# Keys and values of the latent attention by three passes over high and low halves, and two search rounds moved

## The reference, cut to what matters

```python
q, c, qi, ki, wi = jnp.split(h @ w_in, ATT_IN_SPLITS, axis=-1)   # c: 512 x 128, the latent
c = rms_norm(c, kv_norm_g)
score = einsum('bqh,bqhs->bqs', wi, relu(einsum('bqhd,bsd->bqhs', qi, ki)))  # causal
_, idx = lax.top_k(score, 128)                 # 128 keys for every query
logits = (q @ w_uk) @ c[idx] * 64**-0.5 + bias  # 16 heads, softmax over the chosen keys
o = (softmax(logits) @ c[idx]) @ w_uv ; out = o @ w_o
```

## Time and profile before

| | |
|---|---|
| median of three runs | 1879.57 us (1879.13 to 1879.93) |
| the profiled execution, its own time | 1879.85 us |
| its span, first to last instruction | 1878.6 us |
| mean granted TensorE clock | 0.999 |
| TensorE busy | 1859.6 us (99%) |
| VectorE busy | 977.0 us (52%) |
| ScalarE busy | 674.3 us (36%) |
| GpSimd busy | 379.9 us (20%) |

### The profile page before, as it was taken

How to read it: one execution, slowest core, us unless ns; L and a number is a source line. 1 busy time by engine, 2 the same in 40 slices (tenths; PEclk the granted TensorE clock), 3 DMA queues, 4 the chain that set the end, 5 groups by cost and what they waited for, 6 DMA issues and landing times.

```text
span 1878.6 us, 21854 instructions
## 1 busy us (share of the span) xinstructions
PE 1859.6 (99%) x8896; PEld 1505.6 (80%) x8900; DVE 977.0 (52%) x1318; ACT 674.3 (36%) x912; POOL 379.9 (20%) x339
## 2 busy tenths in 40 slices
PE   9999999999999999999999999999999999999998
PEld 8888888888877568888888878788787888888887
DVE  7885533334458864543434347666446454443432
ACT  6753322222234772321212334555323332222213
POOL 2004210010336793210101131111001311110103
PEclk9999999999999999999999999999999999999999
DMA  4323322322322103223223222222232322233221
GB/s 159 113 90 90 112 90 93 109 90 91 107 96 93 66 1 112 90 90 112 90 91 111 76 91 90 68 68 68 84 117 79 112 88 93 90 101 101 90 95 62
DMA packets 167171, 172.36 MB, mean 92 GB/s; under 512 B 7480, under 2 KB 164288, under 8 KB 167072
## 3 DMA queue, kind: packets, MB, share of 16 engines
q1 hardware_dynamic: 164576, 163.76, 26.9%
q0 software_dynamic: 2496, 7.21, 1.2%
HBM read 168.69 MB, written 2.14 MB: 91 GB/s over the span
## 4 chain that ended last, share of the span: by engine, by line
PE 86%; DVE 6%; ACT 4%; issue 2%; DMA 0%; POOL 0%; SPq 0%; DVEq 0%; ACTq 0%
PE bank L775 27%; PE bank L777 27%; PE bank L776 27%; DVE wlo L1700 1%; DVE XC L1802 1%; PE bank L800 1%; ACT whi L1218 1%; PE bank L994 1%; PE bank L1096 1%; PE bank L973 1%; ACT pt L1438 0%; PE bank L922 0%; DVE qe L2106 0%; DMA xtok<-in_x 0%; PE bank L1163 0%
## 5 line engine op out<-in xcount | busy, mean ns | idle before, releaser
L775 PE MATMUL bank<-Ahi,whi 128*128 128x512 f32 (+2 forms) x1416 | 552.8, 390 | 2.5 <-DVE wlo L1700 0.8
L776 PE MATMUL bank<-Alo,whi 128*128 128x512 f32 (+2 forms) x1416 | 547.8, 387 | 0.0
L777 PE MATMUL bank<-Ahi,wlo 128*128 128x512 f32 (+2 forms) x1416 | 547.8, 387 | 0.0
L1700 DVE TENSOR_TENSOR wlo<-stage,whi 128x2048 fp32r<-128x2048 f32 (+2 forms) x146 | 333.1, 2281 | 380.3 <-ACT whi L1218 380.3
L1218 ACT ACTIVATE whi<-stage 128x2048 fp32r<-128x2048 f32 (+2 forms) x152 | 287.1, 1889 | 443.3 <-PE bank L777 443.3
L775 PEld LDWEIGHTS bank<-Ahi,whi 128*128 128x128 f32 (+1 forms) x1416 | 265.3, 187 | 65.6 <-issue 8.2
L776 PEld LDWEIGHTS bank<-Alo,whi 128*128 128x128 f32 (+1 forms) x1416 | 265.4, 187 | 54.9 <-issue 1.2
L777 PEld LDWEIGHTS bank<-Ahi,wlo 128*128 128x128 f32 (+1 forms) x1416 | 265.3, 187 | 55.0
L775 PE MATMUL bank<-Hhi,whi 128*128 128x512 f32 x688 | 267.7, 389 | 0.0
L777 PE MATMUL bank<-Hhi,wlo 128*128 128x512 f32 x688 | 267.6, 389 | 0.0
L776 PE MATMUL bank<-Hlo,whi 128*128 128x512 f32 x688 | 267.6, 389 | 0.0
(11 more groups left out here) (349 smaller groups left out, 2145.4 us busy)
## 6 DMA issues: line engine op xcount, KB each, us to landing
stage<-in_mlp_w_up SPq DMA_DIRECT2D x32, 1024.0 KB, 5.3
stage<-in_mlp_w_down SPq DMA_DIRECT2D x32, 1024.0 KB, 4.9
stage<-in_w_in SPq DMA_DIRECT2D x22, 1024.0 KB, 4.9
stage<-in_w_ffn_in SPq DMA_DIRECT2D x22, 1024.0 KB, 4.9
stage<-in_w_ffn_out SPq DMA_DIRECT2D x8, 1024.0 KB, 5.0
stage<-in_rec_w_in SPq DMA_DIRECT2D x7, 1024.0 KB, 5.1
stage<-in_att_w_in SPq DMA_DIRECT2D x6, 1024.0 KB, 5.3
stage<-in_rec_w_out SPq DMA_DIRECT2D x4, 1024.0 KB, 4.6
```

The lines of the kernel that those rows point to most:

```text
L775: e.matmul(ps, hi, rh, start=first, stop=False)
L776: e.matmul(ps, hi, rl, start=False, stop=False)
L777: return e.matmul(ps, lo, rh, start=False, stop=last)
L1700: e.tensor_tensor(lo_of(u)[:, 0:nk, 0:n], stage[s][:, 0:nk, 0:n], f32(hi_of(u)[:, 0:nk, 0:n]), ALU.subtract).then_inc(s_lo[s], 1)
```

## The change

The latent `cT`, the transposed `w_uk` and the weights `w_uv` get high and low halves, and the 8 key products and the 8 value products go by `three` in place of one 32-bit matmul each. ScalarE makes the high halves: `uvh` (128 x 1024) ahead of the copies of `gv`, `chi` (128 x 512) in step m = 1, and `ukh` (2 x 128 x 512) where it made `ukT`. GpSimd makes `uvl` behind unit 50's low half. VectorE makes `clo` at m = 2 and the two `ukl` at m = 3, after two search rounds; the banks of `uk` are now freed by these two instructions. In the loop over m the rounds are 36 in place of 38, and the two left over go to steps 20 and 21 of the attention, the mask from step 20 to step 22.

```diff
@@ buffers
-    ukT = pool("ukT", 102, [128, 8, 128])
+    chi, clo = pool("chi", 82, [128, S], R), pool("clo", 80, [128, S], R)
+    ukh, ukl = pool("ukh", 102, [128, 8, 128], R), [pool("ukl", kb, [128, 4, 128], R) for kb in (98, 30)]
+    uvh, uvl = pool("uvh", 26, [128, 16, 64], R), pool("uvl", 94, [128, 16, 64], R)
@@ GpSimd, behind lo(50)
+        e.wait_ge(s_uvh, 1)
+        e.tensor_tensor(uvl[:, :, :], w_uv[:, :, :], f32(uvh[:, :, :]), ALU.subtract).then_inc(s_uvl, 1)
@@ TensorE
-        e.wait_ge(s_c, 1)
+        e.wait_ge(s_cl, 1)
         e.wait_ge(*ring.free(("uk", 0)))
         e.wait_ge(*ring.free(("uk", 1)))
         for c in range(8):
             ps = begin(("K", c))
-            e.matmul(ps[:, :], ukT[:, c, :], cT[:, :], start=True, stop=True).then_inc(*ring.put(("K", c)))
+            three(ps[:, :], ukh[:, c, :], ukl[c // 4][:, c % 4, :], chi[:, :], clo[:, :], True, True).then_inc(*ring.put(("K", c)))
...
-                e.wait_ge(s_uv, 16)
-            e.matmul(ps[:, :], cT[:, j * 128:(j + 1) * 128], w_uv[:, 8 * i:8 * i + 8, :].rearrange("p h v -> p (h v)"),
-                     start=True, stop=True).then_inc(*ring.put(("val", j, i)))
+                e.wait_ge(s_uvl, 1)
+            three(ps[:, :], chi[:, j * 128:(j + 1) * 128], clo[:, j * 128:(j + 1) * 128], uvh[:, 8 * i:8 * i + 8, :].rearrange("p h v -> p (h v)"),
+                  uvl[:, 8 * i:8 * i + 8, :].rearrange("p h v -> p (h v)"), True, True).then_inc(*ring.put(("val", j, i)))
@@ ScalarE
         hi(u_of["q", 0] + 1)
+        e.wait_ge(s_uv, 16)
+        e.activation(uvh[:, :, :], w_uv[:, :, :], ACT.Copy).then_inc(s_uvh, 1)
         for i in range(2):
             e.wait_ge(*ring.full(("gv", i)))
...
+            if m == 1:
+                e.wait_ge(s_c, 1)
+                e.activation(chi[:, :], cT[:, :], ACT.Copy).then_inc(s_ch, 1)
             if m == 3:
...
-                    e.activation(ukT[...], ring.bank(("uk", i))[:, :], ACT.Copy).then_inc(*ring.take(("uk", i)))
+                    e.activation(ukh[...], ring.bank(("uk", i))[:, :], ACT.Copy).then_inc(s_ukh, 1)
@@ VectorE, in the loop over m
-            for _ in range((4, 4, 7, 8, 4, 4, 4, 3)[m]):
+            if m == 2:
+                e.wait_ge(s_ch, 1)
+                e.tensor_tensor(clo[:, :], cT[:, :], f32(chi[:, :]), ALU.subtract).then_inc(s_cl, 1)
+            if m == 3:
+                next(search)
+                next(search)
+                for i in range(2):
+                    e.wait_ge(s_ukh, i + 1)
+                    e.tensor_tensor(ukl[i][...], ring.bank(("uk", i))[:, :],
+                                    f32(ukh[...]), ALU.subtract).then_inc(*ring.take(("uk", i)))
+            for _ in range((4, 4, 7, 5, 3, 4, 4, 3)[m]):
                 next(search)
@@ VectorE, in the steps of the attention
-            if t in (2, 5, 8, 10, 12, 14, 16, 17, 18, 19):
+            if t in (2, 5, 8, 10, 12, 14, 16, 17, 18, 19, 20, 21):
                 next(search)
-            if t == 20:
+            if t == 22:
```

More of the change, by code:

```diff
@@ L398, in program @@
     s_osh, s_osl = sem("s_osh"), sem("s_osl")
+    s_ch, s_cl, s_ukh, s_uvh, s_uvl = (sem(n) for n in ("s_ch", "s_cl", "s_ukh", "s_uvh", "s_uvl"))
     s_tsa, s_tsp = sem("s_tsa"), sem("s_tsp")
@@ L1421, in scalar_program @@
                     e.wait_ge(*ring.full(("uk", i)))
-                    e.activation(ukT[:, 4 * i:4 * i + 4, :].rearrange("p a c -> p (a c)"), ring.bank(("uk", i))[:, :], ACT.Copy).then_inc(*ring.take(("uk", i)))
+                    e.activation(ukh[:, 4 * i:4 * i + 4, :].rearrange("p a c -> p (a c)"), ring.bank(("uk", i))[:, :], ACT.Copy).then_inc(s_ukh, 1)
         hi(u_of["wo", 0] + 1)
@@ L1985, in vector_program @@
                     score(2, 4 * m + h)
-            for _ in range((4, 4, 7, 8, 4, 4, 4, 3)[m]):
+            if m == 2:
[6 more added lines that the diff above has]
+                    e.wait_ge(s_ukh, i + 1)
+                    e.tensor_tensor(ukl[i][:, :, :].rearrange("p a c -> p (a c)"), ring.bank(("uk", i))[:, :],
+                                    f32(ukh[:, 4 * i:4 * i + 4, :]).rearrange("p a c -> p (a c)"), ALU.subtract).then_inc(*ring.take(("uk", i)))
+            for _ in range((4, 4, 7, 5, 3, 4, 4, 3)[m]):
                 next(search)
```

## The result

The changed kernel takes 1888.76 us (median of 6 executions, 1887.66 to 1889.72) against 1879.75 us before (6 executions, 1879.03 to 1880.07). The ratio is 1.0049, with an interval of 1.0039 to 1.0059: 9.0 us slower. The prediction was 1880.7 us, 1877.9 to 1882.8. The profiled execution of the changed kernel took 1889.72 us, with a span of 1888.4 us; it is the slowest of the six, 1.0 us above their median.

What follows compares the result with a forecast made beforehand. TensorE, busy 99% of the span, was taken as the bound. Keys -1.5, values -1.2, `uvh` +1.0, `uk` +2.5, rounds +0.3 gave +1.1 us on the profiled 1879.85; as a median 1880.7 us, range 1877.9 to 1882.8.

Steps and rivals of the forecast that it cites:

- The step that failed: VectorE at m = 2, behind the scaling of `q2`: the subtract `clo` holds VectorE for 0.60 us.
- the part on `uk`: `uk` banks freed by VectorE's `ukl` at m = 3: `q4` starts late, 2.5 us lost (1.9 to 3.0).
- now it is VectorE that is late: VectorE at m = 3: `q3` is scaled from 589.35, where before it waited for TensorE at 587.98.
- The clock, a rival at 0.04: Clock falls in the stall at `q4`; a block at half clock costs some 4.8 us, 1885.5 us; chance 0.04.
- the bound from the earlier trace: End of span: full clock from matmuls' stop at 1871.3 until 1874, a little longer than the forecast 2.5 us stall.
- the forecast stall: TensorE idle at `q4`, waiting for the bank that VectorE's `ukl[0]` frees: 2.5 us.
- `uvh`: ScalarE's copy ahead of `gv` delays `q0`, which takes the bank of `gv0`: 1.0 us lost (0.8 to 1.05).
- The wait at `q4`: First pass of `q4` waits about 2.5 us behind VectorE's `ukl`.
- Keys: Eight key products on TensorE by three passes: 5.44 us in place of 6.95, 1.51 us saved.
- Values: Eight value products by three passes: 1.2 us saved (0.7 to 1.5), about 0.3 lost to a longer wait in step 2.
- Rounds: Two search rounds moved to attention steps 20 and 21: 0.3 us lost through later scaling on GpSimd (0 to 2.8).
- At nothing: `chi` on ScalarE (0.6 us) and `uvl` on GpSimd (2.3 us) lie in idle time and cost nothing.

Runs made afterwards that it cites:

- e2: The changed kernel with GpSimd's low half of unit 51 waiting until `clo` is done, `clo` left in its place: 1883.53 us.
- e1: The changed kernel with `clo` moved to m = 1, behind the scores and ahead of the search rounds: 1884.02 us.
- e11: The changed kernel with `clo` at m = 1, `uvh` behind the copies of `gv`, two search rounds ahead of `ukl`: 1882.70 us.
- e3: The changed kernel with ScalarE's copy `uvh` behind the two copies of `gv` instead of ahead: 1887.12 us.
- e5: The changed kernel with `clo` at m = 1, `uvh` behind `gv`, and `w_uk` transposes, `ukh` and `ukl` at m = 5: 1878.25 us.
- e7: The kernel of e5 with only the keys by three passes, values left as one 32-bit matmul each: 1878.37 us.
- e8: The kernel of e5 with only the values by three passes, keys left as one 32-bit matmul each: 1879.41 us.
- e10: The changed kernel with `clo` at m = 1, `uvh` behind the copies of `gv`, one search round ahead of `ukl`: 1880.18 us.
- e4: The changed kernel with the transposes of `w_uk`, `ukh` and `ukl` at m = 5 instead of m = 3: 1882.77 us.
- e12: The changed kernel with `clo` at m = 1, `uvh` behind the copies of `gv`, three search rounds ahead of `ukl`: 1884.03 us.
- e6: The kernel of e5 with the two search rounds of steps 20 and 21 put back into the loop over m: 1882.30 us.

## Why the prediction was wrong

- *The step that failed: "`clo` comes behind it, a subtract of this size holding VectorE for 665.95 - 665.35 = 0.60 us", in the part on `uk`.* It held it for 4.52 us. The size of the tiles was the same, but not where they lie: the row of 665.35 (`OSl<-bank,OSh` in the earlier trace rows) has one input in PSUM, and `clo` has both in SBUF. GpSimd was reading SBUF beside that row too, without any effect on it. Of the eight such subtracts in that trace seven ran beside GpSimd, at 0.67 to 0.68 us, and one alone, at 0.69:

```profile
663.29 2.47 POOL L698 TENSOR_SCALAR pt<-pt,stat 128x384 f32<-128x384 f32 x2 [0.33 <-DVE stat L2005]
```

  With nothing of GpSimd's beside it, or started ahead of GpSimd's, `clo` takes 0.68 us (`e2`, `e1`). The working put `clo` at about 582, and GpSimd's list of the kernel before has a low half right there, from 580.83 to 585.42. The price of such a meeting was in that trace as well, at 545. The prediction asked this of neither row. VectorE, then GpSimd, of the kernel before:

```profile
545.27 4.08 DVE L1953 SCALAR_TENSOR_TENSOR work<-rel,wit,work 128x256 f32<-128x256 f32 x3 [2.84 <-ACT rel L1399]
```

```profile
543.30 4.59 POOL L564 TENSOR_TENSOR wlo<-stage,whi 128x2048 fp32r<-128x2048 f32 x1 [3.45 <-ACT whi L1218]
...
580.83 4.59 POOL L564 TENSOR_TENSOR wlo<-stage,whi 128x2048 fp32r<-128x2048 f32 x1 [4.19 <-ACT whi L1218]
```

  Three such scores take 4.08 us there. The first alone takes 2.90 us and ends 0.28 us behind GpSimd's subtract; the same form takes 0.48 us at 557.50 after, clear of GpSimd.
- *The consequence that had no step.* The working followed VectorE's delay only to `ukl` and `q4`. A delay of 5 us there also reaches the scaling of `q3`, whose bank the last dots take: 3.9 us. The prediction says of q3's scaling "now it is VectorE that is late" and does not ask who waits for it. This would have cost something without the collision too: 0.6 us, the difference between `q4`'s lateness and its wait in `e1`, `e2` and `e11`.
- *The clock, a rival at 0.04, happened.* "Wrong would be [...] a granted clock under 1.00 around 593" came true. The stalls were longer than forecast: together they leave only 0.79 us of matmuls between 591.37 and 598.15. But the bound from the earlier trace rows fails by itself too. There the clock fell some 3 us behind the last matmul; here it fell 1.9 us behind it, and with the forecast stall alone it fell in the profiles of `e1` and `e11`, after the matmuls had gone on. Its price is 2.45 us here and 1.2 to 1.6 us with the forecast stall, not 4.8: the block of 24 passes was not at half clock to its end. The trace before, in which the prediction found no such fall, has no stall of this length either: from 100 to 1800 us TensorE's longest wait is 1.3 us.
- *`uvh`:* 1.0 forecast, 0.96 measured in the ledger, and 1.6 between the medians of `e3` and of the changed kernel. This step was right.
- *The wait at `q4`:* 2.5 forecast, 2.07 behind the late dots and 2.38 without the collision. The mechanism was right, and the wait too; the cost was 3.0, by the 0.6 us above.
- *Keys:* 1.51 forecast, 1.42 measured (5.53 us from `K0` to the first logits in place of 6.95).
- *Values: 1.2 forecast, 0.4 measured by step 8, and 0.2 in the end (`e5` against `e7`).* The bound of 0.7 did not hold. Steps 0 and 1 are each 0.17 us shorter, the full price. In step 2 the transposes wait 0.63 us for GpSimd in place of 0.30. From there the steps follow the way over VectorE, ScalarE and GpSimd, and TensorE's saving goes into its waits. The prediction applied this to the first three values only. `e8` (1879.41) agrees: values alone bring 0.3 us by the medians, which is within the noise.
- *Rounds:* 0.3 forecast, 0.1 measured. At nothing: `chi` and `uvl` cost nothing on TensorE, as forecast. But beside `uvl` the same thing happened to VectorE as with `clo`: a score of 128 x 384 with two SBUF inputs took 2.30 us in place of 0.62. VectorE had the slack there, and that is luck; the prediction did not ask.
- *The range:* with the terms' own ends as the prediction states them the sum is 1879.2 to 1882.4, not 1879.0 to 1882.6, and for the rounds it uses 0.9 where its text gives 2.8 as the upper bound. Neither reaches the measured time.

Put together with the measured sizes but without the collision: -1.4 - 0.2 + 1.0 + 3.0 + 0.1 + 1.4 (the clock, most of the time) = +3.9 us, 1883.7 us. `e1` and `e2`, which are this kernel, have 1884.0 and 1883.5. The collision with its further wait and longer fall costs about 5 us (1888.76 - 1883.53). So without the failed step the forecast would still have been 2.8 to 3.3 us too low and outside its range, by the clock, by the values and by the last dots.

## What to carry to other kernels

Before pricing a VectorE instruction with two SBUF inputs, look at what GpSimd does at that time: its price is then the rest of GpSimd's instruction plus its own, and it delays all behind it. Put it where GpSimd reads nothing, or ahead of GpSimd's instruction, or give it a PSUM input. And take its price from a row with its inputs in the same memories, not only of the same size. Follow a delay to every bank that the engine frees behind it, not to the one that the edit touches. And count a stall of TensorE of about 2 us or more with a surcharge for the clock (1.2 to 1.6 us here behind a single stall); one of 1 us had none.

## What the runs showed of the hardware

- A VectorE subtract of 128 x 512 from two SBUF tiles takes 0.68 us alone and 4.52 us when it starts 0.6 us into a 4.58 us subtract of GpSimd's. GpSimd's does not get longer (4.59 without it, in `e1`).
- With the order turned, GpSimd pays: its 128 x 128 mask takes 0.61 us in place of 0.29 when it starts 0.23 us into `clo`, and `clo` keeps its 0.68 us.
- A VectorE subtract of the same size with one input in PSUM takes 0.68 us beside a GpSimd instruction on SBUF (665.35 of the kernel before).
- In the profiled executions the clock stays at 1.00 behind a wait of 1.06 us (`e10`), falls with one of 1.93 us (`e4`) and of 3.63 us (`e12`), and does either at about 2.4 us: it falls in `e1` and `e11` (2.38), not in `e2` (2.38) and `e6` (2.45). In `e4` and `e11` it falls when the matmuls are running again. At the start of the changed kernel's profiled execution it also falls, at 9.6 us, as TensorE goes on behind a wait of 1.71 us for `x`.
- The clock stays down for some 3.4 us in `e4`, `e11` and `e12`, where TensorE works without a break behind the stall, and for some 10 us in the changed kernel, where two stalls with 0.79 us of dots between them come first.
- The cost of a stall thus rises by a step where the clock begins to fall, and not in proportion: 0.9 us more wait cost 0.6 us, the next 1.3 cost 2.5, the next 1.25 cost 1.3.
